# A two-layer decoder trunk on one core: x loaded by feature pairs, the first weight slab started chunk by chunk

## The reference

```
x = x + short_conv_mixer(rms_norm(x, a_norm), a_w_in, a_conv, a_w_out)   # layer 0
    # bcv = h @ w_in (1024 -> 3072); u = conv3(c_gate * v); (b_gate * u) @ w_out
x = x + squared_relu_mlp(rms_norm(x, mlp_norm[0]), w_up[0], w_down[0])
k, v = shared_kv(x, ...)
x = x + diff_attention(rms_norm(x, b_norm), k, v, ...)                   # layer 1
x = x + squared_relu_mlp(rms_norm(x, mlp_norm[1]), w_up[1], w_down[1])
```

## Time and profile before

| | us |
|---|---|
| median of 3 runs | 1165.77 (1165.45 to 1167.9) |
| span of the profiled execution | 1164.3 |
| PE busy in it | 1148.2 (99%) |
| DVE / ACT busy | 634.3 / 382.6 |
| PE's first matmul of slab 0 starts at | 14.89 |
| mean granted clock of TensorE over the span | 0.997 |

### The profile page before, as it was taken

The page is one execution under the profiler, slowest core; times in us unless marked ns, Lnnn a source line. Parts: engine busy times, 40 slices in busy tenths (PEclk is TensorE's granted clock), DMA queues, the critical chain, the costliest instruction groups (busy, mean ns, idle before and its releaser), DMA issues.

```text
span 1164.3 us, 14392 instructions
## 1 busy us (share of the span) xinstructions
PE 1148.2 (99%) x5432; PEld 948.5 (81%) x5432; DVE 634.3 (54%) x873; ACT 382.6 (33%) x586; POOL 119.0 (10%) x94
## 2 busy tenths in 40 slices
PE   7999999999999999999999999999999999999998
PEld 5888888888888888888888788788888888888887
DVE  5656555643543543555553799946643544544542
ACT  6212233321221221234432677735322222222221
POOL 0000012000000000012210355524000000000000
PEclk8999999999999999999999999999999999999999
DMA  5433333233233233232322111113433233233232
GB/s 149 111 104 95 109 91 101 81 108 109 76 106 109 77 104 108 78 101 94 108 91 73 42 32 37 37 40 98 116 107 109 75 108 108 73 108 109 73 95 86
DMA packets 201557, 105.77 MB, mean 91 GB/s; under 512 B 12576, under 2 KB 196896, under 8 KB 201504
## 3 DMA queue, kind: packets, MB, share of 16 engines
q1 hardware_dynamic: 200464, 105.03, 31.6%
q10 hardware_dynamic: 1040, 0.00, 0.0%
HBM read 102.93 MB, written 2.10 MB: 90 GB/s over the span
## 4 chain that ended last, share of the span: by engine, by line
PE 96%; DVE 2%; DMA 1%; ACT 1%; issue 1%; SPq 0%; ACTq 0%; DVEq 0%
PE ps L427 82%; PE ps L548 8%; PE ps L578 1%; PE ps L605 1%; PE ps L452 1%; DMA kv<-in_x 1%; PE ps L591 1%; PE ps L612 0%; PE ps L581 0%; PE ps L562 0%; DVE nmax L1190 0%; DVE work L1202 0%; PE ps L527 0%; DVE ah L1209 0%; PE ps L516 0%
## 5 line engine op out<-in xcount | busy, mean ns | idle before, releaser
L427 PE MATMUL ps<-h,w_hi 128*128 128x512 f32 x1792 | 557.5, 392 | 3.0 <-DVE h L978 2.6
L427 PEld LDWEIGHTS ps<-h,w_hi 128*128 128x128 f32 x1792 | 334.7, 189 | 71.3 <-issue 2.8
L427 PE MATMUL ps<-h,w_lo 128*128 128x512 f32 x896 | 349.8, 390 | 0.0
L427 PE MATMUL ps<-ah,w_hi 128*128 128x512 f32 x1024 | 315.9, 390 | 0.0
L738 ACT ACTIVATE w_hi<-w_raw 128x1024 fp32r<-128x1024 f32 x185 | 193.3, 1052 | 253.9 <-DMA w_raw<-in_w_up 110.7
L973 DVE TENSOR_TENSOR w_lo<-w_raw,w_hi 128x1024 fp32r<-128x1024 f32 x185 | 232.6, 1261 | 54.9 <-ACT w_hi L738 54.3
L427 PEld LDWEIGHTS ps<-ah,w_hi 128*128 128x128 f32 x1024 | 191.8, 188 | 39.7
L427 PE MATMUL ps<-ah,w_lo 128*128 128x512 f32 x512 | 199.3, 389 | 0.0
L427 PEld LDWEIGHTS ps<-h,w_lo 128*128 128x128 f32 x896 | 168.8, 188 | 35.7
L984 DVE TENSOR_TENSOR xT<-ps,xT 128x512 f32<-128x512 f32 x80 | 55.2, 690 | 205.4 <-PE ps L427 205.4
L796 ACT ACTIVATE ah<-work 128x512 fp32r<-128x512 f32 x64 | 40.5, 632 | 239.7 <-DVE work L1074 239.7
(11 more groups left out here) (105 smaller groups left out, 635.9 us busy)
## 6 DMA issues: line engine op xcount, KB each, us to landing
w_raw<-in_w_up SPq DMA_DIRECT2D x64, 512.0 KB, 4.0
w_raw<-in_w_down SPq DMA_DIRECT2D x64, 512.0 KB, 3.9
w_raw<-in_a_w_in SPq DMA_DIRECT2D x24, 512.0 KB, 3.7
w_raw<-in_w_kv SPq DMA_DIRECT2D x16, 512.0 KB, 3.5
w_raw<-in_a_w_out SPq DMA_DIRECT2D x8, 512.0 KB, 3.9
w_raw<-in_w_q SPq DMA_DIRECT2D x8, 512.0 KB, 4.0
w_raw<-in_w_o SPq DMA_DIRECT2D x8, 512.0 KB, 4.0
kv<-in_x SPq DMA_DIRECT2D x4, 512.0 KB, 6.0
```

Source lines behind the costliest of these rows:

```text
L427: last = nc.tensor.matmul(ps[:, bank, :], w[:, s, k * P:(k + 1) * P], src(half, k), start=(k == 0 and i == 0), stop=(k == KC - 1 and i == 2))
```

## The change

1. **Loads.** x comes in four loads by pairs of feature chunks: each brings 256 features of all 512 tokens (512 KB in packets of 1 KB; before, 128 tokens of all features in packets of 4 KB). Slab 0 comes in two halves of 256 KB. The order is x pair 0, slab 0 first half, x pair 1, slab 0 second half, x pairs 2 and 3, slab 1, slab 2 (which waits as before), then the taps.
2. **PE.** Eight fp32 matmuls of the identity with itself go into PSUM bank 0 before the wait for x. Then transposes of chunks 0 to 3, slab 0's chunks 0 and 1, transposes 4 and 5, slab chunks 2 and 3, transposes 6 and 7, slab chunks 4 to 7. Each chunk has a PSUM bank of its own (banks 4, 5, 6, 7, 2, 3, then 4 and 5 again, for which PE waits until ACT has copied them out).
3. **ACT and DVE.** h_hi and h_lo of the first product read the transposed chunk from PSUM, not from `xT`. ACT makes all eight copies to `xT`: two after the fourth h_hi and six after `split(1)`, which now comes after the eighth. DVE makes no copy. Slab 0 is split in two halves, placed between the chunks.

The diff (declarations of semaphores left out):

```
+X_BANK = (4, 5, 6, 7, 2, 3, 4, 5)
...
@@ -267,18 +270,24 @@
             def cols(w, c):
                 return w[:, :, c * P:(c + 1) * P]
 
-            def load_x(t):
-                sp.dma_start(x_tok[:, t, :], x_d[:, t, :]).then_inc(s_x[t], 16)
-
-            for t in range(TB - 1):
-                load_x(t)
+            def load_x(c2):
+                two = slice(c2 * 2 * P, (c2 + 1) * 2 * P)
+                sp.dma_start(x_tok[:, :, two], x_d[:, :, two]).then_inc(s_x[c2], 16)
+
+            load_x(0)
+            sp.dma_start(w_raw[:, 0, 0:4 * P].rearrange("p (k c) -> p k c", k=4),
+                         win_d[:, 0:4, KC * P:(KC + 1) * P]).then_inc(s_w0, 16)
+            load_x(1)
+            sp.dma_start(w_raw[:, 0, 4 * P:8 * P].rearrange("p (k c) -> p k c", k=4),
+                         win_d[:, 4:8, KC * P:(KC + 1) * P]).then_inc(s_raw[0], 16)
+            load_x(2)
+            load_x(3)
 
             for j in range(KC):
                 for i, part in enumerate((1, 2, 0)):
-                    load(S_IN + 3 * j + i, cols(win_d, part * KC + j))
-                    if j == 0 and i == 0:
-                        load_x(TB - 1)
-                    if j == 0 and i == 1:
+                    if j or i:
+                        load(S_IN + 3 * j + i, cols(win_d, part * KC + j))
+                    if j == 0 and i == 2:
                         with nc.allow_non_contiguous_dma(reason="conv taps: one float a feature"):
                             sp.dma_start(conv[:, :, :], a_conv.rearrange("l w (k p) -> p (l w) k", p=P)).then_inc(s_conv, 16)
                 if j == 2:
@@ -457,20 +466,45 @@
                 spread(BC, lambda t: rcol[:, i, t:t + 1].to_broadcast([P, P]), s_nbc)
 
 
+            def transpose_x(c):
+
+                pe.wait_ge(s_x[c // 2], 16)
+                if c >= 6:
+                    pe.wait_ge(s_xa, c - 5)
+                    pe.wait_ge(s_lo, c - 5)
+                for t in range(TB):
+                    last = nc.tensor.transpose(ps[:, X_BANK[c], t * P:(t + 1) * P], x_tok[:, t, c * P:(c + 1) * P], ident[:])
+                last.then_inc(s_xt, 1)
+
+            def first_slab(k):
+                if k == 0:
+                    pe.wait_ge(s_w0lo, 1)
+                if k == 4:
+                    wait_slab(S_IN)
+                return product(0, S_IN, operand(I_A), (k,), chunks_of(I_A))
+
             pe.wait_ge(s_zero, 5)
             pe.wait_ge(s_cst, 5)
-            for t in range(TB):
-                pe.wait_ge(s_x[t], 16)
-                for hf in range(2):
-                    for k in range(4):
-                        c = (4 * hf + k) * P
-                        last = nc.tensor.transpose(ps[:, 2 * t + hf, k * P:(k + 1) * P], x_tok[:, t, c:c + P], ident[:])
-                    last.then_inc(s_xt, 1)
-            pe.wait_ge(s_xd, TB - 1)
-            pe.wait_ge(s_xa, TB + 1)
-
-            for n in range(N_IN):
-                dense(S_IN + n, U_IN + n, I_A, n == 0)
+            for _ in range(8):
+                nc.tensor.matmul(ps[:, 0, 0:P], ident[:], ident[:], start=True, stop=True)
+            for c in range(4):
+                transpose_x(c)
+            for k in range(2):
+                first_slab(k)
+            for c in range(4, 6):
+                transpose_x(c)
+            for k in range(2, 4):
+                first_slab(k)
+            for c in range(6, KC):
+                transpose_x(c)
+            for k in range(4, KC):
+                last = first_slab(k)
+            last.then_inc(s_used, 1)
+
+            for n in range(1, N_IN):
+                if n == 2:
+                    pe.wait_ge(s_xa, KC)
+                dense(S_IN + n, U_IN + n, I_A)
                 if n == 1:
                     norm_sums(NORM_A)
                 if n == 2:
@@ -750,22 +784,32 @@
                 act.wait_ge(s_nbc, count)
                 nc.scalar.activation(rB[:], ps[:, BC, :], ACT.Copy).then_inc(s_rB, 1)
 
-            for t in range(TB):
-                if t == TB - 1:
-                    split(0)
-                    act.wait_ge(s_xt, 2 * t + 1)
-                    nc.scalar.activation(xT[:, 0:4, t * P:(t + 1) * P],
-                                         ps[:, 2 * t, :].rearrange("p (k q) -> p k q", k=4), ACT.Copy).then_inc(s_xa, 1)
-                act.wait_ge(s_xt, 2 * t + 2)
-                nc.scalar.activation(xT[:, 4:8, t * P:(t + 1) * P],
-                                     ps[:, 2 * t + 1, :].rearrange("p (k q) -> p k q", k=4), ACT.Copy).then_inc(s_xa, 1)
+            def x_hi(c):
+
+                act.wait_ge(s_xt, c + 1)
+                nc.scalar.activation(h1[:, 0, c, :], ps[:, X_BANK[c], :], ACT.Copy, scale=gains[:, g_a, c:c + 1]).then_inc(s_hi, 1)
+
+            def x_copy(c):
+                act.wait_ge(s_lo, c + 1)
+                nc.scalar.activation(xT[:, c, :], ps[:, X_BANK[c], :], ACT.Copy).then_inc(s_xa, 1)
+
             act.wait_ge(s_gain_a, 16)
-            act.wait_ge(s_xd, TB - 1)
-            act.wait_ge(s_xa, TB + 1)
-            for m in range(KC):
-                chunk_hi(I_A, m, g_a)
-                if m == 5:
-                    split(1)
+            x_hi(0)
+            act.wait_ge(s_w0, 16)
+            nc.scalar.activation(w_hi[:, 0, 0:4 * P], w_raw[:, 0, 0:4 * P], ACT.Copy).then_inc(s_w0hi, 1)
+            x_hi(1)
+            x_hi(2)
+            act.wait_ge(s_raw[0], 16)
+            nc.scalar.activation(w_hi[:, 0, 4 * P:8 * P], w_raw[:, 0, 4 * P:8 * P], ACT.Copy).then_inc(s_whi, 1)
+            x_hi(3)
+            x_copy(0)
+            x_copy(1)
+            for c in range(4, KC):
+                x_hi(c)
+            split(1)
+            for c in (4, 5, 2, 3, 6, 7):
+                x_copy(c)
+            act.wait_ge(s_xa, KC)
             for m in range(KC):
                 square(NORM_A, m)
             for n in range(N_IN):
@@ -998,18 +1042,24 @@
             mixed[0] += 1
             dve.wait_ge(s_zero, 3)
             V.tensor_copy(identb[:], ident[:]).then_inc(s_cst, 1)
-            for t in range(TB - 1):
-                dve.wait_ge(s_xt, 2 * t + 1)
-                V.tensor_copy(xT[:, 0:4, t * P:(t + 1) * P],
-                              ps[:, 2 * t, :].rearrange("p (k q) -> p k q", k=4)).then_inc(s_xd, 1)
-            split(0)
+            def x_lo(c):
+                dve.wait_ge(s_hi, c + 1)
+                V.scalar_tensor_tensor(h1[:, 1, c, :], ps[:, X_BANK[c], :], gains[:, g_a, c:c + 1],
+                                       h1[:, 0, c, :].bitcast(F32), ALU.mult, ALU.subtract).then_inc(s_lo, 1)
+
             dve.wait_ge(s_gain_a, 16)
-            dve.wait_ge(s_xd, TB - 1)
-            dve.wait_ge(s_xa, TB + 1)
-            for m in range(KC):
-                chunk_lo(I_A, m, g_a)
-                if m == 5:
-                    split(1)
+            x_lo(0)
+            dve.wait_ge(s_w0hi, 1)
+            V.tensor_tensor(w_lo[:, 0, 0:4 * P], w_raw[:, 0, 0:4 * P], w_hi[:, 0, 0:4 * P].bitcast(F32),
+                            ALU.subtract).then_inc(s_w0lo, 1)
+            x_lo(1)
+            x_lo(2)
+            dve.wait_ge(s_whi, 1)
+            V.tensor_tensor(w_lo[:, 0, 4 * P:8 * P], w_raw[:, 0, 4 * P:8 * P], w_hi[:, 0, 4 * P:8 * P].bitcast(F32),
+                            ALU.subtract).then_inc(s_wlo, 1)
+            for c in range(3, KC):
+                x_lo(c)
+            split(1)
 
             for m in range(KC):
                 dve.wait_ge(s_sq, m + 1)
```

More of the change, by code:

```diff
@@ L175, in build @@
         h_of = [h1, h2, h1, h2, h1, h2, h1]
-        s_x = [sem(f"s_x{t}") for t in range(TB)]
+        s_x = [sem(f"s_x{c2}") for c2 in range(KC // 2)]
+        s_w0 = sem("s_w0")
+        s_w0hi = sem("s_w0hi")
+        s_w0lo = sem("s_w0lo")
         s_gain_a = sem("s_gain_a")
@@ L189, in build @@
         s_xt = sem("s_xt")
-        s_xd = sem("s_xd")
         s_xa = sem("s_xa")
```

## The result

| | before | after |
|---|---|---|
| median of 20 runs, us | 1166.45 (1165.45 to 1167.9) | 1168.12 (1166.51 to 1169.18) |
| span of the profiled execution, us | 1164.3 | 1166.6 |

The ratio is 1.0013, with a 95% interval of 1.0007 to 1.0019: the kernel became 1.5 us slower (0.8 to 2.2), where 1.5 us faster was forecast, and the median (1.7 above that of before) lies above the range. The first three runs of before had a median of 1165.77; over 20 it is 0.7 higher, so that much of the distance to the forecast time is not the change's.

The account below looks back on a forecast made before the run. PE, busy 99% of the span, was taken as the bound. Slab 2 earlier (-2.9), half clock (+1.4) and loads (0) gave -1.5 us, so a span of 1162.8 and a median of 1164.3 us, range 1162.0 to 1167.2.

Parts of the forecast that it names:

- Part 1: PE's start: eight identity matmuls take 3.6 us at half clock, end at 5.7, and later transposes run at full clock.
- Parts 2 and 6: PE's order and the loads: chunk 0 in PSUM at about 6.5, no cost from transposes' clock or later loads.
- Part 3: ACT's list up to the squares: 10.7 us of work plus 1.2 of waits, first square at 18.4 against 18.98.
- Part 4: Squares to slab 2: 7.7 us instead of 8.47, so PE takes slab 2 at 26.2, 2.9 us earlier.
- Part 5: PE idles about 3 us of 4 behind slab 1; half clock around slab 2 costs 1.4 us, bounds 0 and 2.5.
- The sum: Whole kernel: -2.9 for earlier slab 2, +1.4 for half clock, 0 for loads, giving -1.5 us.
- the signs that I named: Trace times: first h_hi 6.3 to 6.9, first square 17.8 to 19.2, slab 1's end 21.5 to 23.5, slab 2's start 25.5 to 27.
- Everything keeps its distance: After slab 2: the order is as before, so the shift of -1.5 us carries unchanged to the end.
- Rival A: Around slab 2: clock holds or is back by 26.2; -2.9 to -3.7 us, 1162.1 to 1162.9; chance 0.18.
- Rival B: Loads: 1 KB packets bring pair 3 and slab 1 2.4 us too late for ACT; 1166.7 to 1167.8; chance 0.16.
- Rival C: PE's start: identity matmuls don't raise the clock in time, transposes take double; 1165.0, up to 1166; chance 0.11.
- Rival D: Slab 1's 6 us earlier start carries through, the wait for `split(2)` being misjudged; -6.0 us, 1159.8; chance 0.03.

Follow-up runs that it names:

- e1: The changed kernel with a two-column activation ahead of ACT's first waits, so the table load comes at the start; 1165.31 us, ratio 0.9995.
- e11: e7 without the early activation, so the table load comes late, behind ACT's wait for chunk 0; 1163.27 us, ratio 0.9971.
- e2: The changed kernel with identity matmuls filling PE's gap behind slab 1, nine before the norm sums and two after; 1164.84 us, ratio 0.9987.
- e3: The changed kernel without the eight identity matmuls at the start; 1168.32 us, ratio 1.0014.
- e5: The kernel before with only the eight identity matmuls added ahead of PE's wait for x; 1166.48 us, ratio 1.0001.
- e8: e7 without the eight identity matmuls at the start; 1163.00 us, ratio 0.9972.
- e9: e7 with four identity matmuls at the start instead of eight; 1161.81 us, ratio 0.9966.
- e4: The changed kernel with slab 2 split ahead of the squares, norm sums after slab 2 and norms spread within slab 3; 1166.28 us, ratio 0.9995.
- e6: The changed kernel with the edits of e1 and e2 together, early table load and filled gap; 1163.67 us, ratio 0.9980.
- e7: The changed kernel with e1's early table load, e4's order, and slab 5 split ahead of the row scales; 1161.28 us, ratio 0.9958.
- e10: The kernel before with only e7's order behind slab 1, its loads and start unchanged; 1166.63 us, ratio 1.0000.
- e12: e7 run again unchanged, as a repeat; 1161.57 us, ratio 0.9957.

## Why the prediction was wrong

- **Part 1 held.** The matmuls of the identity ended at 5.93 (5.7 forecast) at the half-clock rate of the first transposes; chunk 0 was in PSUM at 6.50 (6.5). **Parts 2 and 6 held** as far as they bear on the sum: the transposes of pairs 1 to 3 ran at full clock (eight of them in 1.03 to 1.09 us), and no load of x or of slab 1 is on the chain.
- **Part 3 failed, by a term that was not in it.** The sum 10.7 + 1.2 us from ACT's first h_hi to the first square was right (7.87 to 19.65: 11.8). But it began at 7.87, not at 6.5, and so ended at 19.65, not at 18.4. Before, the table load lay in ACT's idle time at 1.24, ahead of its first wait; in the new order it stands on the chain, behind the wait for chunk 0. The row was in the trace of before and I read it as part of the idle start. The change moves ACT's first activation behind another wait, and I didn't ask what goes with it. e1 and e11 show the size, 1.2 to 1.4 us.
- **Part 4 held.** 7.8 us from the first square to the end of w_lo of slab 2, 7.7 forecast. Shifted by the table load, slab 2 came 1.55 us earlier instead of 2.9.
- **Part 5 had the mechanism and too small a size.** PE idled behind slab 1 (23.8 to 26.0), and the clock was half over slab 2. I took 1.4 us between bounds of 0 and 2.5; it cost 2.8 in the trace of after, for the fall came only during the norm sums, at 26.5, and 5.8 of the 6.8 us at half clock lay over slab 2. The reason given for the small size, that part of the stretch would lie over the gap, held for 1.0 us of it only (1.7 in e1, where the fall came at 25.1 and slab 2 took 8.05). The norm sums themselves took 1.44 us instead of 0.79, which cost nothing: they ended at 27.47, and w_lo of slab 2 at 27.46. The upper bound was set from 4.9 us of matmuls in such a stretch of 6.8, when it should have been from the whole stretch. e2 shows this cost by filling the gap. The size is a matter of the run: in e3's trace the same fall cost 1.7 (7.35 against 5.61), near what I took.
- **The sum.** -1.55 + 2.78 = +1.2, where -1.5 was forecast. The 2.7 us between are the two steps above: 1.35 that slab 2 came later than forecast, which is the table load, and 1.4 of the half clock. Of the signs that I named, the first h_hi, the first square, the end of slab 1 (23.8) and the start of slab 2 (27.60) all fell outside their ranges, each on the late side; the pause of PE and the half clock came as named.
- **"Everything keeps its distance" failed too.** It held from slab 3 to 730 us (1.2 us at both places); then the attention stage lost 1.1 us to a second stretch at half clock in the profiled run. Its waits were there before. By the clocks, most runs of after (16 of 20, at 0.995 and 0.996) have more half clock than slab 2 alone accounts for; of the 77 runs of before whose clocks are listed beside the experiments, four are as low (1166.9 to 1167.6), and eight more of 1166.8 to 1167.8 stand at 0.999 and 1.000, which the mean clock doesn't explain. Where the extra half clock lies, a mean can't say. The traces with a stretch in the attention stage are after, e1, e5, e8, e9 and e11; before, e2, e3, e4, e6, e7, e10 and e12 have none. So neither the new start (e2, e3) nor the identity matmuls (absent in e8) nor the late table load (absent in e1) makes it by itself. Why it comes in some runs stays open.
- **Rival A** (the clock holds) is what e2 makes; it gave 1164.84 with the table load still late. **Rival B** had the right sign for a wrong reason: the loads were never late for ACT, whose only wait between the first h_hi and the squares was for PE's transposes (1.0 us at 14.48); the chain does not hold a load. The first square at 19.65, near the 19.9 from which this rival has the kernel slower, came from the table load. **Rival C** falls: the transposes of pair 1 took 1.09 us, full clock. **Rival D** was nearer than it looked: 4.9 us of its 6.0 were there to be had (e7), but behind `split(2)` stood `split(5)` too (e4).

In the trace of after the clock was at 1.00 until 26.5, fell while PE did the norm sums after 2.2 us without work, and was back at 33.4 within slab 2. The Trainium skill (TensorE: Matmul & The Clock Gate, "Why this matters for your kernels") warns against idle gaps of PE between bursts of matmuls, because they bring the clock back to half. In kind after and e2 agree with it; the gap that the page names is longer than the 2.26 us that PE's timeline has in after, where the clock fell, and e4's gap of 2.25 us left the clock at 1.00.

## What to carry to other kernels

An earlier start only pays as far as the next thing in line is earlier too: read each engine's order down to the place where PE first waits for something it didn't wait for, and look for the items there that stand ahead of the next weights without being needed (e7). A gap opened on PE can cost more than its length, since the work behind it may run at half clock: 1.7 to 2.8 us of slab 2 in the traces of e3 and after, for 2.3 us without work. Filling it took this away (e2, e6). And look where ACT's table load stands when the first activation moves: in after it had come behind a wait that it didn't need (e1).

## What the runs showed of the hardware

- The load of ACT's table takes 1.28 us. In before, where one wait for a semaphore stands ahead of the first activation, it began at 1.24, and the activation only at 6.54; in after, where two stand ahead of it (for the gains and for chunk 0), it began at 6.57, behind both. That it is the number of waits which decides isn't shown; no run moves the one wait alone. An activation of two columns ahead of them had it at 1.27 (e1).
- Matmuls of the identity with itself in fp32 kept the granted clock at 1.00 over a gap (e2 and e6, 23.0 to 28.0) although the array only multiplies zeros and ones.
- The clock that the windows print for the first microseconds (1.00) was not the engine's: eight transposes took 1.97 us at 8.16 in e3, where the windows print 1.00, and 1.09 to 1.10 in after and e7 at the same place in the program.
- Stretches at half clock aren't tied to a kernel: over slab 0 the profiled run of before has 6.8 us of it and those of e5 and e10 3.4; at slab 2 that of after has 6.8 and that of e3 3.4.
